# Expert gate and up matrices as eight rows a partition instead of two groups of four

## The reference, cut to what matters

```
h   = rmsnorm(x, norm2) * (1 + sc2) + sh2
grp = argmax(h @ wg + bg);  top_i = top2(h @ we + be, within grp)
y_e = (silu(h @ w1[e]) * (h @ w3[e])) @ w2[e]      # w1, w3: 1024 x 512, w2: 512 x 1024
x   = x + g2 * sum over the token's two experts of weight * y_e
out = rmsnorm(x, norm_f)
```

## Time and profile before

| | us |
|---|---|
| median of 3 runs | 1754.91 (1751.19 to 1756.32) |
| the profiled execution's own time | 1753.52 |
| its span | 1751.6 |
| PE busy | 1628.7 (93%) |
| DVE busy | 646.8 (37%) |
| ACT busy | 406.9 (23%) |
| POOL busy | 176.3 (10%) |

### The profile page before, as it was taken

The page is one execution under the profiler, slowest core; times in us unless marked ns, Lnnn a source line. Parts: engine busy times, 40 slices in busy tenths (PEclk is TensorE's granted clock), DMA queues, the critical chain, the costliest instruction groups (busy, mean ns, idle before and its releaser), DMA issues. The chain is left out here.

```text
span 1751.6 us, 37114 instructions
## 1 busy us (share of the span) xinstructions
PE 1628.7 (93%) x16025; PEld 1069.8 (61%) x16025; DVE 646.8 (37%) x1594; ACT 406.9 (23%) x908; POOL 176.3 (10%) x220
## 2 busy tenths in 40 slices
PE   5999999999999998999999999999999999998783
PEld 3444445898777786644444445556777767666562
DVE  3533332001767666766655455561000000000003
ACT  4000000001666666610010003221121122111112
POOL 1205000000111110000000000001111111111100
PEclk9999999999999999999999999989999999999996
DMA  9874224131011107334452172169999999999996
GB/s 341 258 230 112 74 84 146 37 104 42 2 44 44 33 2 237 111 111 129 120 145 83 37 280 85 68 258 390 391 383 384 394 387 382 396 392 397 406 385 229
DMA packets 146623, 356.07 MB, mean 203 GB/s; under 512 B 14751, under 2 KB 94231, under 8 KB 121851
## 3 DMA queue, kind: packets, MB, share of 16 engines
q1 hardware_dynamic: 120656, 305.50, 47.0%
q0 software_dynamic: 12656, 28.01, 6.0%
q10 hardware_dynamic: 13148, 20.18, 3.3%
HBM read 320.53 MB, written 45.36 MB: 209 GB/s over the span
## 5 line engine op out<-in xcount | busy, mean ns | idle before, releaser
L2635 PE MATMUL psum<-sb_m_xT,sb_m_ring 128*64 128x64 f32 (+2 forms) x4096 | 152.0, 235 | 22.0 <-issue 17.7
L2635 PEld LDWEIGHTS psum<-sb_m_xT,sb_m_ring 128*64 128x64 f32 x4096 | 147.8, 140 | 35.6 <-issue 34.7
L2384 ACT ACTIVATE sb_m_xT<-psum,sb_rowmod 128x64 f32<-128x64 f32 (+2 forms) x256 | 81.7, 424 | 216.3 <-PE psum L2623 216.3
L2519 DVE TENSOR_TENSOR sb_m_hT<-psum,sb_m_sg 128x256 f32<-128x256 f32 (+2 forms) x32 | 15.3, 477 | 308.9 <-PE psum L2635 308.9
L748 PE MATMUL psum<-sb_vD,sb_room 128*128 128x512 f32 x240 | 104.7, 593 | 0.2 <-DVE sb_vD L685 0.2
L2635 PE MATMUL psum<-sb_m_xT,sb_front 128*64 128x64 f32 (+2 forms) x2560 | 94.5, 236 | 9.9 <-issue 7.3
L2635 PEld LDWEIGHTS psum<-sb_m_xT,sb_front 128*64 128x64 f32 x2560 | 92.4, 142 | 17.2 <-issue 16.9
L1008 ACT ACTIVATE sb_d_probs<-sb_d_probs,sb_d_nmax 128x640 f32<-128x640 f32 (+7 forms) x128 | 92.9, 735 | 1.6 <-DVE sb_d_nmax L1048 1.0
L2642 PE MATMUL psum<-sb_m_ring,sb_m_hT 128*64 128x512 f32 (+2 forms) x256 | 84.5, 611 | 5.6 <-DMA sb_m_ring<-in_exp_w_dram 4.7
L780 PE MATMUL psum<-sb_b_wvd,sb_rows 128*128 128x256 f32 x384 | 88.9, 394 | 0.0
L780 PEld LDWEIGHTS psum<-sb_b_wvd,sb_rows 128*128 128x128 f32 x384 | 84.9, 286 | 3.3
(11 more groups left out here) (384 smaller groups left out, 2408.8 us busy)
## 6 DMA issues: line engine op xcount, KB each, us to landing
sb_m_ring<-in_exp_w_dram SPq DMA_DIRECT2D x48, 2048.0 KB, 34.4
sb_front<-in_exp_w_dram SPq DMA_DIRECT2D x30, 2048.0 KB, 33.8
sb_rows<-in_exp_w_dram SPq DMA_DIRECT2D x18, 2048.0 KB, 36.5
sb_g_ada<-in_ada_w_dram SPq DMA_DIRECT2D x16, 1024.0 KB, 5.3
d_qk<-sb_n_b_sel ACTq DMA_DIRECT2D x20, 512.0 KB, 3.2
sb_front<-in_w_in_dram SPq DMA_DIRECT2D x16, 512.0 KB, 5.4
sb_front<-d_qk SPq DMA_DIRECT2D x15, 512.0 KB, 7.5
sb_n_b_sel<-in_w_in_dram SPq DMA_DIRECT2D x10, 512.0 KB, 8.9
```

What stands on the lines that cost most here:

```text
L2384: last = act.activation(dst[:, kk, 0:w], src, ACT.Identity, scale=k.rowmod[:, 0, kk:kk + 1], bias=k.rowmod[:, 1, kk:kk + 1])
L2635: mm = pe.matmul(k.psum[part, which, c * w:(c + 1) * w], view[:, kk, first:first + 2 * CAPS - 1:2], x[:, kk, 0:w], start=(kk == 0), stop=( ...
```

## The change

Four edits belong together.

1. `expert_matrix` lays gate and up matrices out with eight consecutive rows a partition: partition p gets rows 8p to 8p+7, one piece of 16 KB. Down matrices stay as they are. It is used by the two loads in `stage_out` (block 0) and by the 62 in `stage_moe`.
2. `rowmod` (scale and shift by partition and group) follows this order: one run of 8 values a partition instead of two of 4.
3. `turn` takes every eighth column instead of every fourth. A narrow block now has 8 transposes, each of 64 token rows by 128 columns, which write 64 columns each; `modulate` reads them from there, 8 instructions as before.
4. Narrow blocks gather whole rows of 4 KB into 64 partitions, by a new index tile `idx_row` that DVE makes once. `idx_small` stays, since the adds into `d_sum` still use half rows.

```
-    return slot.rearrange("p (h c) -> p h c", h=2), w[0, e].rearrange("e (h p q) n -> p (e h) (q n)", h=2, p=P)
+    return slot.rearrange("p (h c) -> p h c", h=1), w[0, e].rearrange("e (p q) n -> p e (q n)", p=P)
...
-                sp.dma_start(k.rowmod[:, i, :].rearrange("p (h q) -> p h q", h=2),
-                             k.d_mod[i].rearrange("(h p q) -> p h q", h=2, p=P)).then_inc(s_rowmod, 16)
+                sp.dma_start(k.rowmod[:, i, :], k.d_mod[i].rearrange("(p q) -> p q", p=P)).then_inc(s_rowmod, 16)
...
+        idx_row = sb("idx_row", [CAPS, NE - NBIG], I32)
...
-                    pool.indirect_dma_start(xg[b % 2][:, 0:BANK], None, halves,
-                                            bass.IndirectOffsetOnAxis(ap=idx_small[:, r - NBIG:r - NBIG + 1], axis=0),
-                                            bounds_check=2 * S - 1, oob_is_err=False).then_inc(s_g[b % 2], 16)
+                    pool.indirect_dma_start(xg[b % 2][0:CAPS, :], None, k.d_xn,
+                                            bass.IndirectOffsetOnAxis(ap=idx_row[:, r - NBIG:r - NBIG + 1], axis=0),
+                                            bounds_check=S - 1, oob_is_err=False).then_inc(s_g[b % 2], 16)
...
-                           k.psum[:, 2, (kk % 4) * P + CAPS * (kk // 4):(kk % 4) * P + CAPS * (kk // 4 + 1)])
+                           k.psum[:, 2, kk * CAPS:(kk + 1) * CAPS])
...
+            v.inc(dve.tensor_copy(idx_row[:, :], real[0:CAPS, 2 * NBIG:UNITS])); v.wait(dve)
...
-                for kk in range(KD if w > CAPS else KD // 2):
-                    first = kk // 4 * BANK + kk % 4
-                    tr = pe.transpose(k.psum[:, 2 + kk // 4, (kk % 4) * P:(kk % 4 + 1) * P],
-                                      src[:, first:first + 4 * (P - 1) + 1:4], k.ident)
+                for kk in range(KD):
+                    cols = slice(kk, kk + KD * (P - 1) + 1, KD)
+                    if w > CAPS:
+                        tr = pe.transpose(k.psum[:, 2 + kk // 4, (kk % 4) * P:(kk % 4 + 1) * P], src[:, cols], k.ident)
+                    else:
+                        tr = pe.transpose(k.psum[:, 2, kk * CAPS:(kk + 1) * CAPS], src[0:CAPS, cols],
+                                          k.ident[0:CAPS, 0:CAPS])
```

More of the change, by code:

```diff
@@ L2293, in _ @@
         def _(pool):
-            halves = k.d_xn.rearrange("s (h d) -> (s h) d", h=2)
             sums = k.d_sum.rearrange("s (h d) -> (s h) d", h=2)
```

## The result

The kernel after takes 1772.06 us (median of 6 runs, 1768.25 to 1775.82) against 1754.58 us of the kernel before in the same comparison (6 runs): a ratio of 1.0094 [1.0081, 1.0107], about 16.5 us more. The prediction said 1750 us, with a range of 1741 to 1764. The sign was wrong, and the time lies outside the range.

The account below looks back on a forecast made before the run. The prediction took the DMA engines to bound the experts, with PE close behind. Loads -5.2 us, gathers 0, PE 0 (covered) and the rest 0 gave -5.2 us from the median of 1754.9, rounded to 1750 us, range 1741 to 1764.

Parts of the forecast that it names:

- What bounds the kernel: Experts run at the pace of the DMA engines, share 1.00; PE close behind, with 15.0 us of waits for weights.
- The gathers: Narrow gathers as whole rows: nothing left to save, 0, at most 0.7 us; later landing covered up to 14 us latency.
- The loads: 62 gate and up loads, 7936 pieces fewer at 10.4 ns each: 5.2 us less, between nothing and 8.1 us.
- PE: Four more transposes in 19 narrow turns: 9.1 us, covered by PE's waits for weights, so 0.
- The rest: DVE's index copy, `rowmod` loads, ACT and DVE work: 0, at most 0.2 us if block 1's gather were late.
- A: PE becomes the bound through dearer eightfold-step turns: slower, +9.1 us, 1764, or +27.1 us, 1782; chance 0.17.
- B: Longer load pieces gain nothing, fixed cost an artefact or runs cut again: no change, 1755 us; chance 0.20.
- C: 16 KB load pieces move more slowly, 5% beyond their bytes: +16 us, 1771; chance 0.08.
- D: More is gained: 16.3 ns a piece plus 0.7 us of gathers, or less queue contention: -9 us, 1746; chance 0.12.

Follow-up runs that it names:

- e3: Kernel after with the narrow gathers of before (half rows into 128 partitions), output wrong; 1755.39 us, 1.0000 of before.
- e7: Kernel before with the 12 wide gathers after the first issued over all 128 partitions instead of 112 or 80; 1741.26 us, 0.9919 of before.
- e2: Kernel after with gate and up loads in 8 KB pieces as in before, output wrong; 1769.52 us, 1.0084 of before.
- e5: Kernel after with narrow whole-row gathers issued over 128 partitions, tokens on partitions 0 to 31 and 96 to 127; 1756.18 us, 1.0002 of before.
- e6: Kernel after with narrow gathers issued over 128 partitions, tokens still on 0 to 63, other indices out of bounds; 1757.66 us, 1.0018 of before.
- e1: Kernel before with only the gate and up loads in 16 KB pieces, output wrong; 1755.26 us, 1.0003 of before.
- e12: e7 with gate and up loads in 16 KB pieces, output wrong; 1738.61 us, 0.9914 of before.
- e4: Kernel after with two 8 KB pieces for each 16 KB one, same HBM places, halves swapped in SBUF; 1772.07 us, 1.0091 of before.
- e9: Kernel after with each narrow gather as two gathers of 2 KB half rows into the same 64 partitions; 1777.05 us, 1.0117 of before.
- e8: e7 with the wide adds into the sum also issued over 128 partitions; 1750.51 us, 0.9971 of before.
- e11: e5 with wide gathers and wide adds also issued over 128 partitions; 1749.98 us, 0.9972 of before.

## Why the prediction was wrong, step by step

**What bounds the kernel** held. The stage runs at the pace of the DMA engines: e3 adds 19 x 4 transposes at no cost that can be told, and where the rate rises (e7) or falls (after) the time follows. But "DMA share 1.00" was read as "the engines do all they can". They were busy 1.02 of the time at 378, 392, 400 and 403 GB/s alike. The share says that they are busy, not how much they move.

**The gathers is the step that failed.** It read: "Whole rows have nothing left to save there: 0". I priced what the new gather would save or cost on its own, its engine time from the earlier trace rows, its latency, its cover. Of that the cover held: its issue takes 0.98 us, its last packet comes 2 us later than before (8.8 for 6.8 us behind the issue), far inside the 14 us that were allowed, and no wait of PE stands before a narrow turn. Its engine time did not: 9.6% of 134.4 us are 12.9 us for the gather above, where the earlier trace rows gave 9.9. What I didn't price is what a gather of another shape does to the transfers beside it. It costs them 16.5 us in 19 gathers, 0.87 us each; e2, e3, e5 and e6 show it to be this. The row that would have given it away stands in the trace of before: from 1210 to 1370 us the stretches of 8 us beside wide gathers, issued over 112 partitions, ran at 374 to 389 GB/s, and those beside narrow gathers, over 128, at 415 to 423. A wide gather also moves more bytes, so that row alone would have been a warning and no proof; e7, which changes the partitions and not the bytes, is the proof. I had bounded the unseen operation, a gather over 64 partitions, from a row of one over 128, although gathers over fewer were there to be read.

**The loads** were priced at -5.2 us, from 10.4 ns a piece. Measured are 4.3 ns in e1 and 10.7 in e12, in times nothing that can be told. The interval of e1 leaves out 5.2 us; that of e12 against e7 does not. So this term was mis-sized in the kernel as it was, by 3 to 5 us, and its lower bound of nothing fits the times as well as anything; what a piece costs when the gathers disturb nothing stays open. The three rows of the line differ in contention as well as in size. The Trainium skill's account in "DMA: Bandwidth & Descriptors", section "Why small descriptors are slow (HBM only)", from which the prediction worked out an estimate of 4.7 ns and 2.3 us, agrees with the 4.3 ns of e1 and not with the 10.7 of e12.

**PE** was right: 0, covered. The narrow turn came out at 1.09 us, under the 1.23, so the four transposes more cost 0.34 us a turn and not 0.48, and the eighth column is no dearer than the fourth.

**The rest** was right: the index copy is one instruction of 0.17 us,

```profile
1187.24 0.17 DVE L2508 CAST sb_m_idx_row<-sb_m_real 64x19 int32<-64x19 f32 x1
```

1.3 us ahead of the gather of block 1, and e3, which keeps it, has the time of before.

**The rivals.** A (PE, 1764) is excluded by the turns and e3. B (the pieces don't gain) is true of the loads, and was not the whole. C (long pieces are slower, 1771) came nearest in time and had the right sign in the profile, a dearer byte on q1. It was wrong in its cause: e1 has the long pieces and no loss, e2 and e4 the loss without them. The prediction also misread the row that it weighed for C. In the earlier trace rows the two queues have 55.6% and 47.0%, 102.6% in sum, so their packets hardly overlapped, and the 69 ns are not to be halved; but q1, with shorter pieces, had 0.470 x 80 / 0.54 = 70 ns in the same stretch. Both were slow there, so the row says nothing against long pieces. A rival in which the gather slows the loads was missing. "Less contention between the queues" stood in D, with the opposite sign only.

## What to carry to other kernels

Where the DMA engines are saturated, compare bytes a second and not their busy share, and do it in stretches: beside each kind of small transfer, and away from all. A small indirect gather can cost the large loads beside it more than its own bytes, so price a change of its shape by the rate around gathers of both shapes in the trace before. Beside saturated loads, as here, issue a gather over all 128 partitions, with indices out of bounds where there is no row; try the same on accumulating adds before trusting it there.

## What the runs showed of the hardware

- A gather of 0.25 MB over 64 partitions beside saturated loads holds the core at 379 GB/s for the 8 us from its issue (319 to 328 while its packets move); a wide one over 112 or 80 partitions at 376. Over 128 partitions the narrow one has 418 to 421 and the wide one 418 (e7). The target addresses carry about 3 of the 16.5 us, 5 at the end of the interval (e6 against before), and the length of the rows, 2 or 4 KB, none of the loss (e9).
- What makes the difference inside the DMA engines no run here shows, since the trace doesn't say which engine carries which row. The Trainium skill, "DMA: Bandwidth & Descriptors", section "The descriptor swizzle", describes how a transfer to 128 partitions is laid out so that each DMA engine writes one port of SBUF. That a gather of fewer partitions loses this layout would fit the runs; it is argued, not shown.
- Out-of-bounds rows of a gather leave small packets (1286 more on q0 in e6 than in after from 1210 to 1680 us, 64 a gather of them for these rows) and cost no time that can be seen (e5, 1.0002 [0.9990, 1.0013]).
- Accumulating adds over 128 partitions for 112 or 80 made the kernel slower, by 8 to 9 us for 13 of them (e8, e11). The loss does not show beside these adds (378 and 380 GB/s), and its cause stays open.
- Transposes that pick every eighth fp32 column load their weights in 193 to 203 ns (medians), every fourth in 212, neighbours in 141: there is a price for a step, and no further one for the longer step.
